# Inverse square roots in a two-layer decoder kernel: ScalarE square root and VectorE reciprocal in place of ScalarE logarithm and exponential

## The reference

```python
def rmsnorm(x, g, eps=EPS):                       # before each sublayer, of the memory, at the end
    y = xf * lax.rsqrt(jnp.mean(xf * xf, axis=-1, keepdims=True) + eps)
    return (y * g.astype(jnp.float32)).astype(x.dtype)

kk = kk / jnp.maximum(jnp.sqrt(jnp.sum(kk * kk, axis=-1, keepdims=True)), 1e-12)   # RWKV keys
y = ((y - mean) * lax.rsqrt(var + RWKV_LN_EPS)) * lnx_w + lnx_b                    # RWKV group norm
o = rmsnorm(o, onorm).reshape(B, S, VW) * jax.nn.silu(og)                          # GLA, per head
```

## Time and profile before

| | |
|---|---|
| median of 3 runs | 2093.97 us (2093.78 to 2095.69) |
| profiled execution | 2091.24 us, span 2089.5 us |
| busy: PE, VectorE, ScalarE, GpSimd | 94%, 30%, 22%, 8% of the span |
| mean granted TensorE clock | 0.964 of full speed |
| DMA | 466 MB, mean 223 GB/s |

### The profile page before, as it was taken

The page is one execution under the profiler, slowest core; times in us unless marked ns, Lnnn a source line. Parts: engine busy times, 40 slices in busy tenths (PEclk is TensorE's granted clock), DMA queues, the critical chain, the costliest instruction groups (busy, mean ns, idle before and its releaser), DMA issues.

```text
span 2089.5 us, 21780 instructions
## 1 busy us (share of the span) xinstructions
PE 1958.5 (94%) x8283; PEld 970.1 (46%) x8283; DVE 618.6 (30%) x1029; ACT 455.8 (22%) x759; POOL 166.3 (8%) x201
## 2 busy tenths in 40 slices
PE   7999989999978999999998999989968999999997
PEld 3555888746453333333333444734453333333333
DVE  2153776432131232223223004201241223123223
ACT  2254332232211111111112004502311111111112
POOL 2000454100001000000000000300000000000000
PEclk9999998999968999999999999999968999999998
DMA  6210100034027999999993122103037999999991
GB/s 172 81 41 6 36 1 1 1 103 199 3 119 303 427 427 428 427 427 428 428 416 146 42 70 91 40 0 161 3 121 321 427 427 428 428 427 427 428 416 46
DMA packets 70222, 466.24 MB, mean 223 GB/s; under 512 B 20378, under 2 KB 22538, under 8 KB 45594
## 3 DMA queue, kind: packets, MB, share of 16 engines
q1 hardware_dynamic: 58592, 448.87, 52.3%
q10 hardware_dynamic: 6682, 8.25, 1.2%
q0 software_dynamic: 4896, 8.40, 1.1%
HBM read 468.64 MB, written 6.29 MB: 227 GB/s over the span
## 4 chain that ended last, share of the span: by engine, by line
PE 67%; DMA 25%; DVE 4%; ACT 2%; issue 1%; SPq 0%; POOL 0%; DVEq 0%; ACTq 0%; POOLq 0%
PE ps L962 63%; DMA W<-in_moe_w 24%; PE ps L1142 1%; PE ps L1481 1%; DVE XI L1771 1%; DVE HT L1596 0%; DMA xin<-in_x 0%; PE ps L1507 0%; SPq L396 0%; DVE XJ L1767 0%; DMA xg<-hrows,idc 0%; PE ps L1079 0%; ACT L665 0%; PE ps L1343 0%; PE ps L1454 0%
## 5 line engine op out<-in xcount | busy, mean ns | idle before, releaser
L962 PE MATMUL ps<-W,xgT 128*64 128x512 f32 x2048 | 456.2, 598 | 9.9 <-DMA W<-in_moe_w 5.5
L962 PE MATMUL ps<-HT,W 128*128 128x512 f32 (+1 forms) x896 | 399.3, 604 | 18.8 <-DVE HT L1596 10.4
L962 PEld LDWEIGHTS ps<-W,xgT 128*64 128x64 f32 x2048 | 144.6, 138 | 294.6 <-issue 278.1
L962 PEld LDWEIGHTS ps<-HT,W 128*128 128x128 f32 (+1 forms) x896 | 170.4, 192 | 235.4 <-issue 222.5
L1994 DVE TENSOR_TENSOR XT<-ps,XT 128x512 f32<-128x512 f32 x240 | 166.0, 692 | 241.4 <-PE ps L962 241.4
L962 PE MATMUL ps<-W,act 128*64 128x512 f32 x1024 | 232.3, 595 | 2.8 <-ACT ysb L925 2.8
L962 PE MATMUL ps<-spread,ysb 128*128 128x512 f32 x512 | 228.3, 599 | 3.2 <-ACT ysb L925 3.2
L1986 DVE TENSOR_TENSOR act<-ps,sl 128x256 f32<-128x256 f32 x64 | 26.9, 421 | 450.9 <-ACT sl L920 450.9
L962 PEld LDWEIGHTS ps<-spread,ysb 128*128 128x128 f32 x512 | 94.6, 190 | 136.5 <-issue 136.5
L916 ACT ACTIVATE hs<-ps 128x512 f32<-128x512 f32 x64 | 38.3, 598 | 443.8 <-PE ps L962 443.8
L962 PEld LDWEIGHTS ps<-W,act 128*64 128x64 f32 x1024 | 70.8, 137 | 136.4 <-issue 136.4
(11 more groups left out here) (358 smaller groups left out, 1773.8 us busy)
## 6 DMA issues: line engine op xcount, KB each, us to landing
W<-in_moe_w SPq DMA_DIRECT2D x192, 2048.0 KB, 17.1
W<-in_od_w_in SPq DMA_DIRECT2D x6, 2048.0 KB, 8.0
W<-in_ev_w_in SPq DMA_DIRECT2D x3, 2048.0 KB, 8.0
W<-in_xa_wq SPq DMA_DIRECT2D x2, 2048.0 KB, 9.1
W<-in_xa_wo SPq DMA_DIRECT2D x2, 2048.0 KB, 7.9
hrows<-hk ACTq DMA_DIRECT2D x8, 512.0 KB, 2.7
W<-in_od_w_out SPq DMA_DIRECT2D x2, 2048.0 KB, 7.8
W<-in_ev_w_in SPq DMA_DIRECT2D x2, 1024.0 KB, 13.7
```

What stands on the lines that cost most here:

```text
L962: return te.matmul(o, l, r, start=first, stop=last)
```

## The change

Every logarithm and exponential pair becomes one square root on ScalarE and a reciprocal on VectorE, placed directly ahead of the operation that uses the result. In the GLA loop the reciprocal stands at the end of VectorE's part of a chunk, behind a new wait for the root (`g_root`), and it is what now releases GpSimd (`g_rs`). The ScalarE side of the GLA loop is written out for four chunks instead of being a loop of the engine.

```diff
-                inverse_root(rs[:, 0:width], ps[:, 7, 0:width], D, 0).then_inc(s["rstd_ready"], 1)
-            def inverse_root(dst, src, count, eps, sem=None, value=None):
-                ins = sc.activation(dst, src, ACT.Ln, bias=cst[:, eps:eps + 1], scale=1.0 / count)
...
-                return sc.activation(dst, dst, ACT.Exp, scale=-0.5)
+                root(rs[:, 0:width], ps[:, 7, 0:width], D, 0).then_inc(s["rstd_ready"], 1)
+            def root(dst, src, count, eps):
+                return sc.activation(dst, src, ACT.Sqrt, bias=cst[:, eps:eps + 1], scale=1.0 / count)
...
-                st.then(sc.activation(KN[:, :, :], KN[:, :, :], ACT.Ln))
-                sc.activation(KN[:, :, :], KN[:, :, :], ACT.Exp, scale=-0.5).then_inc(s["pre_a"], 1)
+                sc.activation(KN[:, :, :], KN[:, :, :], ACT.Sqrt).then_inc(s["pre_a"], 1)
...
-                inverse_root(At[:, :, :], ps[:, 4:8, :], HD, 1).then_inc(s["post_a"], 1)
+                root(At[:, :, :], ps[:, 4:8, :], HD, 1).then_inc(s["post_a"], 1)
...
-                with act.Fori(0, NCH) as c:
+                for c in range(NCH):
...
-                    inverse_root(grs[:, :, :].rearrange("p h t -> p (h t)"), ps[:, 6, :], 256, 0, s["g_ln"], c + 1).then_inc(s["g_rs"], 1)
+                    root(grs[:, :, :].rearrange("p h t -> p (h t)"), ps[:, 6, :], 256, 0).then_inc(s["g_root"], 1)
...
                 dve.wait_ge(s["rstd_ready"], n["norm"])
+                st.then(ve.reciprocal(rs[:, 0:width], rs[:, 0:width]))
...
                 dve.wait_ge(s["pre_a"], 7)
+                st.then(ve.reciprocal(KN[:, :, :], KN[:, :, :]))
...
                 dve.wait_ge(s["post_a"], 2)
+                st.then(ve.reciprocal(At[:, :, :], At[:, :, :]))
...
+                    dve.wait_ge(s["g_root"], c + 1)
+                    ve.reciprocal(grs[:, :, :], grs[:, :, :]).then_inc(s["g_rs"], 1)
```

More of the change, by code:

```diff
@@ L342, in trunk @@
             "iv_tl", "iv_tr", "iv_u", "iv_ul", "iv_v", "iv_x", "akv_done", "akv_in", "wt_done", "wt_in", "u_done", "u_in",
-            "g_cs", "g_exp", "g_scaled", "g_copied", "g_turned", "g_tok", "g_mat", "g_masked", "g_y", "g_sq", "g_sum", "g_ln", "g_rs",
+            "g_cs", "g_exp", "g_scaled", "g_copied", "g_turned", "g_tok", "g_mat", "g_masked", "g_y", "g_sq", "g_sum", "g_root", "g_rs",
             "g_added", "g_state", "g_half", "g_out",
@@ L888, in odd @@
                     sc.activation(gsq[:, :, :], y, ACT.Square).then_inc(s["g_sq"], 1)
-                    sc.activation(HT[:, :, bass.ds(c * CH, CH)], y, ACT.Copy).then_inc(s["g_sq"], 1)
+                    sc.activation(HT[:, :, c * CH:c * CH + CH], y, ACT.Copy).then_inc(s["g_sq"], 1)
                     act.wait_ge(s["g_sum"], c + 1)
                     act.wait_ge(s["g_out"], c + 1)
-                    inverse_root(grs[:, :, :].rearrange("p h t -> p (h t)"), ps[:, 6, :], 256, 0, s["g_ln"], c + 1).then_inc(s["g_rs"], 1)
+                    root(grs[:, :, :].rearrange("p h t -> p (h t)"), ps[:, 6, :], 256, 0).then_inc(s["g_root"], 1)
                 n["xt"] += 8
```

## The result

| | before | changed |
|---|---|---|
| median | 2093.88 us (2089.74 to 2095.69) | 2141.55 us (2140.29 to 2142.04) |
| span of the profiled execution | 2089.5 us | 2138.5 us |
| mean granted TensorE clock | 0.964 | 0.953 |

The ratio of the times is 1.0228, 95% interval 1.0215 to 1.0241: 47.7 us more. The forecast was 2136, range 2123 to 2149. This part shows where the 49 us between the two spans lie. One thing to set right first: the two MoE stages take some 550 us each in the trace of before, a little over a quarter of the span each, not a little under half.

A forecast was written before the change was run, and what follows sets the result against it. PE was taken to bound the kernel, busy 94% of the span. Terms 8.6 + 3.75 + 12.2 + 9.7 = 34.2, + 8 for the clock = 42 us, gave 2136 us against the median of 2094; range 2123 to 2149.

The forecast's parts named there:

- The price of the reciprocal: On VectorE, 6.25 ns an element: 3353 ns for 128x512, 12.95 us for 128x2048.
- the two rivals on that price: Reciprocal streams when long: 2087 us, 4%; or costs eight plain element times (8.3 ns): 2155 us, 4%.
- Removed and added in a norm: Path from logarithm or root to first scaling: 4.10 us against 2.67, +1.43 at six exposed norms, 8.6 us.
- The norm of cross-attention 0: Costs nothing, since PE multiplies the memory keys for 14 us meanwhile; without that cover 1.43 us.
- No drain behind a table load: The trace disagrees with the skill's 1.38 us drain per load; with it, seven exposed loads would give back 9.7 us more.
- Key norm: Before softmax block 2: the divide of KN delays the block's closing, so PE's transposes start 3.75 us later.
- Group norm: After RWKV: the divide of At delays residual half 5, so PE's last half tile waits; +12.2 us.
- GLA loop: Next chunk's mask queued behind the divide: +2.76 us three times, 8.3, plus 1.43 at the end; sum 9.7 us.
- The clock: TensorE's granted clock falls after new PE gaps: together 8 us, between 2 and 13.
- Loads that the root brings: Exponentials after a root need their own table load, in MoE, cross-attention, before the tanh, layer-1 gate chain; costs nothing.
- only norms exposed: Rival: the three reciprocals outside the norm helper hide beside PE's matmuls; 8.6 + 2, 2105 us, 4%.
- theory B: Experiments' rival for the 48 us: something common to the new code, wherever it stands in the queues; no chance given.

The follow-up runs named there:

- norms_only: The kernel before with root and reciprocal in the norm helper alone (eight norms); ratio to before 1.0070.
- one_set: The kernel before, logarithm and exponential kept, one table set holding both named ahead of each wait, ScalarE's GLA loop written out; 2083.73 us, ratio 0.9949.
- keys_only: The kernel before with root and reciprocal for the RWKV key norm (KN) alone; ratio to before 1.0036.
- four kernels of one part each: The kernel before with root and reciprocal only in the norm helper, key norm, group norm or GLA head norm; ratios 1.0070, 1.0036, 1.0076, 1.0090.
- unroll_only: The kernel before with only ScalarE's GLA loop written out; 2091.55 us against 2093.64, ratio 0.9995.
- the moves: Changed kernel with GLA divide behind next mask (2134.15 us), group-norm divide in four parts (2137.01), key-norm divide behind softmax closing (2137.34); all together 2125.41.
- GLA filler: The changed kernel with four unread 128x512 matmuls per GLA chunk behind the scores; 2137.41 us, ratio to before 1.0211.

## Why the prediction was right

The time, 2141.5 us, is within the range, 5 above the forecast. By its steps:

- **The price of the reciprocal** (6.25 ns an element): exact, 3353 and 12954 ns. With it the two rivals on that price fall. That the line of two small forms held over 500 and 2000 elements was an assumption, and it had only those two points. Nothing streams, and the eight plain element times that the Trainium skill's repeat count suggested ("VectorE: DVE Perf Modes", the hardware resources ahead of its modes) are six in every shape measured. The page gives the count, and neither a duration nor a word on streaming; to read it as eight plain operations was my own step.
- **Removed and added in a norm** (2.67 to 4.10, six exposed, 8.6 us): the path is 4.11. The first norm alone is longer: four small preparations stand ahead of the divide in VectorE's queue. Before, they lay beside the exponential; now they lie in the path. The divide starts at 26.31 and the scaling at 29.70, while the root started at 24.98: 4.72 us, 2.0 more than before instead of 1.4. PE's waits for the six norms grew by 8.9 us, where the forecast has 8.6. Their stretches grew by 10.2, with the clock's share in it; the forecast has 8.6 and 1.7 for the layer-1 norm. That this sum fits so well is partly luck: the first norm and MoE 0 are above their 1.4, and MoE 1 is far below (0.3, and 0.1 in norms_only), though its path is 4.10 us as well. In both MoE stages PE's wait behind the routing (10.0 us, for `bhot`) ends 1.4 to 1.5 us later after the root than before, as forecast; MoE 0 then takes another 1.1 us longer and MoE 1 is back by 1.1 in the expert loop, where nothing was changed. What does that was not tried. The norm of cross-attention 0 cost nothing, as worked out.
- **No drain behind a table load.** Of the 1.38 us in the Trainium skill's "ScalarE: Activation LUTs" (what ACT_TABLE_LOAD costs) one_set shows nothing either. Without the exposed load a norm's path shortens from 2.67 to 1.38, by 1.29, which is the load's 1283 ns alone.
- **Key norm** (+3.75): the wait is 3.77 in the timeline. The stretch grew by 7.2 us here and by 8.6 in keys_only. The clock is the step that was too small: I took 1.0 us with 1.7 as its bound. The window of the changed kernel behind that wait, where before had 1.00 in the same work:

```profile
172.00:182.00 10.00, 6.73 (x20) 4.78 (x21) 4.16 (x4) 2.37 (x2) 0.00 (x0) 0.50 0.00 0
```

  Ten microseconds at half the clock, of which PE worked 6.7: 3.4 us of work at the full clock became 6.7, so 3.4 were lost. 3.8 + 3.4 = 7.2 is the whole stretch.
- **Group norm** (+12.2, and 2.4 for the clock): 14.4, and the wait of 12.03 is ahead of the last half tile, as foreseen.
- **GLA loop** (2.76 per mask, a period of 12.8): the masks made PE wait 10.9 - 3.1 = 7.8 us more, where the forecast has 8.3. The period is 14.3 and once 15.4, because each gap also brings 1.6 to 2.7 us of clock. I took 1.0, and 1.7 as the bound, the loss in one window of before. One such loss is no bound: this one and the key norm's went beyond it.
- **The clock** (8, between 2 and 13): this is the term that was mis-sized. The waits came out as forecast, 33.9 us against 34.2. What is left of the 47.5 us (the growth without the RWKV stretch) is some 13, at the upper bound, and PE's busy time grew by 13.4 us with the same matmuls. By stretch it grew by 3.5 at the key norm (1.0 taken), 2.4 at the group norm (2.4), 6.0 in the three GLA chunks (3.0), and 0.5 at the layer-1 norm (1.7). Behind that last norm the clock did fall:

```profile
1167.00:1172.00 5.00, 4.31 (x5) 1.85 (x6) 5.00 (x8) 0.00 (x0) 0.00 (x0) 0.50 0.00 0
```

  But further on in the same stretch it was low for a shorter time than before (0.57 over the 4 us from 1291.0, where before had 0.51 over the 7 us from 1258.9), so only 0.5 was left of the loss. Here too the small difference is chance as much as forecast.
- **Loads that the root brings** (nothing): borne out, as far as a stretch can tell. The table loads fell from 41 to 24 in all. In MoE 0 the exponential of the routing has a load of its own now, and PE's next wait ends 1.46 us later after the root than before, which is the norm's part alone. The stretches of cross-attention grew by 0.0 and 1.2.

Of the rivals, "only norms exposed" (2105) is excluded by the four kernels of one part each, and theory B by unroll_only and by the moves: the same instructions in another order gave 16 us back.

## What to carry to other kernels

Price a reciprocal on VectorE by its element count before moving work to it, and then look at what is queued behind it: here an instruction of 3.35 or 12.95 us costs mostly what PE's next releaser is late, and moving it behind that releaser recovers the part that is order. Count the clock behind a gap of PE besides its length: in this kernel the key norm, the group norm and the GLA masks (gaps of 3.4 to 12 us) lost 1.6 to 3.5 us more each, and a single trace in which a gap went unpunished was no evidence against that. Before replacing a function for the sake of its table loads, ask whether one set serves both and can be loaded while the engine waits: that line was worth 10 us here where the replacement cost 48.

## What the runs showed of the chip that I had not expected

- The same instruction stream with the same waits got a clock of 0.62 or 0.91 in one stretch, and 0.66 or 1.00 in another, in different executions. It moves a stretch by 1.7 to 4 us each time; single executions of the kernel before spread over 2089 to 2096 us.
- A matmul of 128x512 in float32 is two records, about 0.9 us. My GLA filler was twice as long as I had planned for, and by chance closed the gap entirely.
- A logarithm and an exponential, though one set holds both, got a load each until the set was named.
